# Sparse-attention scores as two rounded products over 128 rows instead of one fp32 product per 64 rows

## The chip, the cores and the metric

The kernel runs on one core of one Trainium2 chip. The metric is the device time of one launch in microseconds (us), the median of several executions. Lower is better.

## The reference

The program is a model of 512 tokens and width 1024, all in fp32. The first block has a gated linear attention layer, a sparse attention layer ("NSA") and a convolutional feed-forward after each. The second block has two layers that mix differential and stick-breaking attention, each with a feed-forward. The change lies in the sparse attention layer, which has 16 query heads in 4 groups, with a head dimension of 64:

```python
q_rot = rope(q, pos)
p_sel = masked_softmax(jnp.einsum('bkgqd,bkqmd->bkgqm', qc, ks) * scale, kpos <= qpos[:, None])
o_sel = jnp.einsum('bkgqm,bkqmd->bkgqd', p_sel, vs)
p_win = masked_softmax(jnp.einsum('bkgqd,bknd->bkgqn', qc, kw) * scale, win_mask)
o_win = jnp.einsum('bkgqn,bknd->bkgqd', p_win, vw)
o = gates[0] * o_cmp + gates[1] * o_sel + gates[2] * o_win
```

At this length the selected blocks and the window both cover every earlier token, so the kernel computes both as plain causal attention, each with keys and values of its own.

## The kernel before, in words

**Weights.** All weight matrices come as a stream of 128x1024 units through a ring of four slots (`w_raw`, filled by SyncE's queue). GpSimd splits each unit (`split`, L496): one cast to the rounded type `w_hi` (L502), then four subtractions of 128x256 that give the remainder `w_lo` (L505). A projection is then three products in the rounded type fp32r: high by high, high by low, low by high (`product`, L544 to L548). For the eight units of the compression network ScalarE does the cast (L1463) and GpSimd only the subtractions. TensorE starts a unit of the attention stages when half of its remainders are there (`unit_rows`, L550).

**The key and value stage** (about 600 to 694 us in the trace) multiplies twelve tiles of 128 columns. VectorE evacuates each (L2116), the four key tiles are rotated (L2133 to L2141, into `n_rot`), and ScalarE writes each half of 64 partitions of a rotated key tile to both halves of the partitions of `n_kk` (`k_doubled`, L1479 to L1485). VectorE also writes the remainders of the next stage's input here (`mixed_low`, L2091). Between the tiles stand the eight compression units (`compress`, L860 to L862). Counted in the order of the stream (`KV_UNIT`, `CMP_UNIT`, L72), units 0 to 6, 8, 10, 12, 14 and 16 are tiles and the rest up to 19 are compression; unit 20 is the first of the query stage.

**The query stage** (694 to about 753 us) multiplies one unit of gates and eight of queries. Each query tile `e` holds two heads, one on partitions 0 to 63 and one on 64 to 127 (`par` 0 and 1). VectorE rotates it into `n_q[:, e]`.

**The score stage** (745 to about 897 us) is a pipeline over 96 score rows. `row(m)` (L207) names each: tile `e = m // 12`, a block of 128 tokens `i`, which of the two sides (selected, window), and the head `par`. Within a tile the rows come in six pairs, by m modulo 12: 0 and 1 have i = 0 and both sides, 256 columns; 2 to 5 have i = 3 and one side, 512 columns; 6 and 7 have i = 1 and both sides, 512 columns; 8 to 11 have i = 2 and one side, 384 columns. For a pair q, q+1:

- TensorE: `scores(q)` (L933) multiplies the two heads' queries with the keys, each on its own 64 rows of the array, in fp32 (L947; every fp32 product is two instructions in the trace), and adds the causal mask (L951). It waits until the exponentials of row q-3 are done (the banks form a ring of four). Then it transposes rows q-4 and q-3 (`transposed`, L953 to L965), each only when the copy of the row three before it has freed its bank (`copied`, L925). At four steps of a tile it multiplies with the values (L1023), once after a product for the compressed part (L1018).
- VectorE, in the order of its loop over q (L2286): copies of odd transposed rows (L2310), the row maximum (L2231), the reciprocal of row q-1's sum (L2237), and now and then other work.
- ScalarE, in its loop (L1578): copies of even transposed rows (L1589, row q-5), the exponentials of row q (L1555), once a tile the rounded output `n_oh` (L1597).
- GpSimd multiplies a row with its gate and reciprocal (`weigh`, L511 to L519) and does no splitting meanwhile.

The order on each engine is written out by hand.

Of the kernel before, what the change touches and what calls it, by code (L numbers as in the profile page):

```python
# [138 lines left out]
def build(nc, x_in, weights, params, consts, masks, gain_out, out):  # L139
    ctx = ExitStack()  # L140
    with ctx:
# [60 lines left out]
        CS_BANK = (6, 7, 6, 0)  # L202
        CMP_TURN_ROW = (22, 58)
        SWAP_ROW = (27, 28, 33, 34, 51, 52, 57, 58)
        PV_ROW = {12 * e + at_: 4 * e + k for e in range(8) for k, at_ in enumerate((10, 12, 14, 16))}
# [40 lines left out]
        def parts_gain(n, k):  # L246
# [50 lines left out]
        o_kh, o_kl = o_A + 4352, o_A + 8448  # L297
        n_kk = at("n_kk", [P, 2, NSA_KV, T], F32, o_kh)
        n_k = [[n_kk[:, c, g, :] for g in range(NSA_KV)] for c in range(2)]
        n_v = [at(f"n_v{s}", [P, TT, NSA_KV * DH], F32, o_A + 12544 + 1024 * s) for s in range(2)]  # L300
# [7 lines left out]

        n_q = at("n_q", [P, 8, T], F32, o_XH)

        n_hid = at("n_hid", [P, 2, 2, P], F32, o_N + 2048)
# [104 lines left out]
            "xh2", "xl2", "kd", "evac", "yh", "yl", "rot", "rope", "vT", "vc", "hid", "kvc", "kvcc", "gT",  # L416
            "gate", "p0", "cs", "csub", "cmax", "ce", "p", "s", "mx", "exp", "w", "t", "tc", "pT", "pTc", "pv", "oh", "o", "rc", "tcd")}
        hs = {n: sem("hyb_" + n) for n in (
# [31 lines left out]
        def _(sp):  # L450
# [13 lines left out]
            rounds = UNITS // RING  # L464
            kv_round, q_round = (START["kv"] + 4) // RING, -(-START["nsa_q"] // RING)

# [12 lines left out]
            refill_rounds(1, kv_round)  # L479
            for u in range(kv_round * RING, q_round * RING):  # L480
                refill(u)
            refill_rounds(q_round, rounds)
            for u in range(rounds * RING, UNITS):
# [11 lines left out]
        def _(pool):  # L495
# [15 lines left out]
            def weigh(m):  # L511
# [7 lines left out]
                ins.then_inc(ns["w"], 1)  # L519

            def split_first():

                for p in range(4):
                    rows, last = slice(2 * p, 2 * p + 2), p == 3
                    if p == 0:
                        pool.wait_ge(s_first_raw, 16)
                    if p == 2:
                        pool.wait_ge(s_raw[0], 16)
                    nc.gpsimd.tensor_copy(w_hi[0][:, rows, :], w_raw[0][:, rows, :]).then_inc(s_hi if last else s_first_hi, 1)
                    pool.wait_ge(s_hi, 1) if last else pool.wait_ge(s_first_hi, p + 1)  # L530
                    nc.gpsimd.tensor_tensor(w_lo[0][:, rows, :], w_raw[0][:, rows, :], w_hi[0][:, rows, :].bitcast(F32),
                                            ALU.subtract).then_inc(s_w if last else s_first_w, 1)

            split_first()
            for u in range(1, UNITS):
                if u == START["nsa_o"] + RING - 1:
                    for m in range(POOL_ROWS, NSA_ROWS):
                        weigh(m)
                split(u)


        @block.tensor
        def _(pe):
# [292 lines left out]
            def nsa():  # L836
# [96 lines left out]
                def scores(q):  # L933

                    e, i, cs, _, n = row(q)
                    S = (i + 1) * P
                    if q >= 4:
                        pe.wait_ge(ns["exp"], q - 2)
                    elif q == 2:
                        pe.wait_ge(ns["csub"], 3)  # L940
                    if q % 12 == 0:
                        pe.wait_ge(ns["rope"], 4 + e + 1)
                    side = slice(cs[0], cs[-1] + 1)
                    for par in range(2):
                        r = slice(DH * par, DH * (par + 1))
# [23 lines left out]
                for t in range(U_NSA_Q):  # L969
# [15 lines left out]
                    if t == 7:  # L985
                        pe.wait_ge(s_bf, 2)
                        pe.wait_ge(ns["kd"], 4)
                        pe.wait_ge(ns["pTc"], 1)
                        scores(0)
# [293 lines left out]
        def _(act):  # L1283
# [163 lines left out]
            def nsa():  # L1447
# [22 lines left out]
                def k_swap(m):  # L1470
                    t = (4, 5, 8, 9)[m]
                    act.wait_ge(ns["evac"], t + 1)
                    if m >= 2:
                        act.wait_ge(ns["kd"], m - 1)
                    half_swap(n_rot[m % 2], n_raw[:, t % 2, :], ns["rot"])

                halves = (slice(0, DH), slice(DH, P))

                def k_doubled(m):  # L1479

                    act.wait_ge(ns["rope"], m + 1)
                    for e, r in enumerate(halves):
                        for to in halves:
                            ins = nc.scalar.activation(n_k[m // 2][2 * (m % 2) + e][to, :], n_rot[m % 2][r, :], ACT.Copy)
                    ins.then_inc(ns["kd"], 1)  # L1485
# [30 lines left out]
                act.wait_ge(ns["kvc"], 1)  # L1516
                act.wait_ge(ns["p0"], 1)
                for par in range(2):
# [23 lines left out]
                def swap(e):  # L1542
                    act.wait_ge(ns["evac"], U_NSA_KV + 1 + e + 1)
                    act.wait_ge(ns["rope"], 4 + e - 1) if e >= 2 else act.wait_ge(ns["kd"], e + 3)
                    half_swap(n_rot[e % 2], n_raw[:, (e + 1) % 2, :], ns["rot"])
# [237 lines left out]
        def _(dve):  # L1783
# [302 lines left out]
            def nsa():  # L2086
# [82 lines left out]
                V.memset(n_bd[:, :, :, :], 0.0).then_inc(ns["p0"], 1)  # L2169
                evac(8)  # L2170
                mixed_low(6)
                evac(9)
# [3 lines left out]
                key(3)  # L2176
                evac(11)

                dve.wait_ge(s_used, CMP_UNIT[-1] + 1)
# [53 lines left out]
                def score_weights(m):  # L2233
# [4 lines left out]
                    if m < POOL_ROWS:  # L2238
# [47 lines left out]
                for q in range(3, NSA_ROWS + 9):  # L2286
# [376 lines left out]
```

## Time and profile before

| | |
|---|---|
| median of 3 executions | 2813.29 us (2812.91 to 2813.4) |
| the profiled execution: its span, first to last instruction | 2810.2 us |
| its own time by the clock of the runs | not noted apart; the median is 3.1 us above the span |
| TensorE busy | 2791.2 us, 99% |
| VectorE, ScalarE, GpSimd busy | 1325.6, 816.3, 2045.0 us |
| granted TensorE clock, mean | 0.999 of full |

Busy times count modelled ends of pipelined matmuls, so an engine at 99% can still be waiting between two starts. The starts in the timeline show that better: the distance from one start to the next is what a matmul really takes from the stream. "idle before" in a row is the time between two spans, and the name behind the arrow is what ended it.

### The profile page before, as it was taken

What the parts mean: (1) busy time and instruction counts of PE and PEld (TensorE: products, weight loads), DVE (VectorE), ACT (ScalarE), POOL (GpSimd) and SP (SyncE); (2) the same over time, 40 slices, a digit from 0 to 9 for tenths busy, and PEclk for the clock granted to TensorE, in tenths of its full rate; (3) what the DMA queues carried; (4) which work ended last, traced back from release to release, by engine and by line L of the source; (5) the groups of instructions that cost most, each with busy time, mean ns of one, the idle gap of its engine ahead of it and who ended that gap; (6) DMA issues with size and microseconds to landing.
All of it is one profiled execution on the core that took longest, in us unless ns stands there. A gap on an engine that the chain in (4) does not pass through costs nothing.

```text
span 2810.2 us, 39309 instructions
## 1 busy us (share of the span) xinstructions
PE 2791.2 (99%) x14380; PEld 2253.4 (80%) x14380; DVE 1325.6 (47%) x1878; ACT 816.3 (29%) x1470; POOL 2045.0 (73%) x2353
## 2 busy tenths in 40 slices
PE   9999999999999999999999999999999999999999
PEld 7888888888766888888877788888887777888887
DVE  4945666044675566604764553321074545432201
ACT  3242222024575222202444422110043444211101
POOL 7958988778654899877845587777785456877774
PEclk9999999999999999999999999999999999999999
DMA  4213323323100333322221233323332222333322
GB/s 154 77 54 105 97 96 94 95 96 128 61 2 8 98 97 97 97 96 91 83 68 61 68 98 98 97 96 93 96 97 70 65 66 77 98 97 95 94 96 96
DMA packets 66507, 242.59 MB, mean 86 GB/s; under 512 B 7504, under 2 KB 7632, under 8 KB 66384
## 3 DMA queue, kind: packets, MB, share of 16 engines
q1 hardware_dynamic: 66384, 240.95, 27.1%
q8 instruction: 78, 1.28, 0.2%
q14 instruction: 45, 0.37, 0.0%
HBM read 238.82 MB, written 2.10 MB: 86 GB/s over the span
## 4 chain that ended last, share of the span: by engine, by line
PE 95%; DVE 2%; ACT 2%; issue 1%; DMA 0%; POOL 0%; SPq 0%; DVEq 0%; ACTq 0%
PE bank L546 28%; PE bank L548 28%; PE bank L547 28%; PE bank L1023 1%; PE bank L947 1%; PE bank L1204 1%; PE bank L1120 1%; PE bank L965 1%; PE bank L1163 1%; PE bank L1176 1%; PE bank L1101 1%; ACT n_P L1555 0%; PE bank L602 0%; PE bank L951 0%; PE bank L1091 0%
## 5 line engine op out<-in xcount | busy, mean ns | idle before, releaser
L505 POOL TENSOR_TENSOR w_lo<-w_raw,w_hi 128x256 fp32r<-128x256 f32 x1780 | 1479.1, 862 | 45.6 <-ACT w_hi L1463 10.6
L546 PE MATMUL bank<-XH,w_hi 128*128 128x512 f32 x2416 | 955.4, 395 | 2.2 <-DVE X L2509 1.6
L548 PE MATMUL bank<-XH,w_lo 128*128 128x512 f32 x2416 | 941.2, 390 | 0.0
L547 PE MATMUL bank<-XL,w_hi 128*128 128x512 f32 x2416 | 940.7, 389 | 0.0
L502 POOL CAST w_hi<-w_raw 128x1024 fp32r<-128x1024 f32 x437 | 486.6, 1114 | 618.0 <-DMA w_raw<-weights_dram 617.4
L546 PEld LDWEIGHTS bank<-XH,w_hi 128*128 128x128 f32 x2416 | 453.6, 188 | 103.1 <-issue 9.3
L548 PEld LDWEIGHTS bank<-XH,w_lo 128*128 128x128 f32 x2416 | 453.4, 188 | 96.3
L547 PEld LDWEIGHTS bank<-XL,w_hi 128*128 128x128 f32 x2416 | 453.8, 188 | 93.4 <-issue 2.6
L1822 DVE TENSOR_TENSOR X<-X,bank 128x512 f32<-128x512 f32 x63 | 43.1, 684 | 511.6 <-PE bank L548 511.3
L548 PE MATMUL bank<-hid_h,w_lo 128*128 (+1 forms) x704 | 273.9, 389 | 0.0
L546 PE MATMUL bank<-hid_h,w_hi 128*128 (+1 forms) x704 | 273.9, 389 | 0.0
L547 PE MATMUL bank<-hid_l,w_hi 128*128 (+1 forms) x704 | 273.9, 389 | 0.0
L1855 DVE TENSOR_TENSOR f_c<-bank,rstd 128x512 f32<-128x512 f32 x88 | 60.9, 692 | 296.5 <-PE bank L548 286.7
L1349 ACT ACTIVATE hid_h<-f_h 128x512 f32 x88 | 55.6, 632 | 392.5 <-DVE f_h L1870 392.5
L547 PEld LDWEIGHTS bank<-hid_l,w_hi 128*128 128x128 f32 x704 | 132.1, 188 | 27.6
L548 PEld LDWEIGHTS bank<-hid_h,w_lo 128*128 128x128 f32 x704 | 132.1, 188 | 27.4
L546 PEld LDWEIGHTS bank<-hid_h,w_hi 128*128 128x128 f32 x704 | 132.1, 188 | 27.3
L518 POOL TENSOR_SCALAR n_P<-n_P,n_st,n_gate 128x512 f32<-128x512 f32 (+3 forms) x124 | 78.7, 639 | 65.8 <-DVE n_st L2237 65.0
L1341 ACT ACTIVATE f_c<-f_u,par_sb 128x512 f32<-128x512 f32 x88 | 71.9, 818 | 168.2 <-DVE f_u L1855 168.2
L1347 ACT ACTIVATE f_s<-f_c 128x512 f32<-128x512 f32 x88 | 55.7, 633 | 197.3 <-DVE f_c L1855 152.3
L1872 DVE TENSOR_TENSOR hid_l<-f_h,hid_h 128x512 f32 x88 | 74.0, 840 | 81.0 <-ACT hid_h L1349 81.0
L1864 DVE SCALAR_TENSOR_TENSOR f_c<-f_u,par_sb,f_c 128x512 f32<-128x512 f32 x88 | 102.6, 1166 | 12.7 <-DVE f_c L1861 0.3
(368 smaller groups left out, 3297.3 us busy)
## 6 DMA issues: line engine op xcount, KB each, us to landing
w_raw<-weights_dram SPq DMA_DIRECT2D x445, 512.0 KB, 3.5
x_tok<-x_dram SPq DMA_DIRECT2D x4, 512.0 KB, 5.4
out_dram<-y_tok SPq DMA_DIRECT2D x4, 512.0 KB, 4.1
const_sb<-consts_dram SPq DMA_DIRECT2D x1, 834.0 KB, 11.8
par_sb<-params_dram SPq DMA_DIRECT2D x1, 665.0 KB, 10.3
masks_in<-masks_dram SPq DMA_DIRECT2D x1, 640.0 KB, 12.9
w_raw<-weights_dram SPq DMA_DIRECT2D x2, 256.0 KB, 6.5
y_gain<-gain_out_dram SPq DMA_DIRECT2D x1, 512.0 KB, 4.5
```

What stands on the lines that cost most here:

```text
L502: nc.gpsimd.tensor_copy(w_hi[s][:, :, :], w_raw[s][:, :, :]).then_inc(s_hi, 1)
L505: ins = nc.gpsimd.tensor_tensor(w_lo[s][:, rows, :], w_raw[s][:, rows, :], w_hi[s][:, rows, :].bitcast(F32), ALU.subtract)
L518: ins = nc.gpsimd.tensor_scalar(w, w, n_st[:, 1, st:st + 1], n_gate[:, i, col:col + 1], ALU.mult, ALU.mult)
L546: nc.tensor.matmul(out_ap, w_hi[slot][:, j, :], xh, start=start, stop=False)
L547: nc.tensor.matmul(out_ap, w_hi[slot][:, j, :], xl, start=False, stop=False)
L548: return nc.tensor.matmul(out_ap, w_lo[slot][:, j, :], xh, start=False, stop=stop)
L1341: nc.scalar.activation(f_c[side][:, :], f_u[side][:, 2:T + 2], ACT.Identity, bias=par_sb[:, bass.ds(t + b0, 1)], scale=par_sb[:, bass.ds(t ...
L1347: nc.scalar.activation(f_s[:, :], f_c[0][:, :], ACT.Silu).then_inc(s_silu, 1)
L1349: nc.scalar.activation(hid_h[:, bass.ds(i * (2 * T) + p * T, T)], f_h[:, :], ACT.Copy)\
L1855: V.tensor_tensor(dst, bank[2 * p + side][:, :], rstd[:, :], ALU.mult).then_inc(s_u, 1)
L1864: V.scalar_tensor_tensor(f, f_u[side][:, 0:T], par_sb[:, bass.ds(c + w0, 1)], f, ALU.mult, ALU.add).then_inc(s_c2, 1)
L1872: V.tensor_tensor(hid_l[:, bass.ds(i * (2 * T) + p * T, T)], f_h[:, :], hid_h[:, bass.ds(i * (2 * T) + p * T, T)].bitcast(F32), ALU.subtract)\
```

## The change

- The keys are kept as two tiles, `n_kh` (rounded, fp32r, written by ScalarE's doubling copy in place of `n_kk`) and `n_kl` (their remainders, written by VectorE, four subtractions of 64x512 for each of four key tiles). ScalarE's half swaps wait for them (`ns["kl"]`).
- The queries of one head are stacked on 128 rows in `n_qs`: GpSimd casts the query tile to both places (`query_parts`, two casts of 128x512 a tile), and VectorE overwrites the other head's 64 rows with this head's remainders (`query_low`, two subtractions of 64x512 a tile).
- A score is then two fp32r products over 128 rows, stacked queries by high keys and stacked queries by low keys, for each of the two heads.
- `query_parts` stands on GpSimd after the splits of the query stage's sixth and eighth unit and before `weigh` of rows 4, 16, 28, 40, 56 and 74. `query_low` stands on VectorE after the rotation of tile 4, after the last evacuation of the query stage, and in its loop at q = 10, 22, 34, 46, 62 and 80.
- SyncE's refills are written out, not looped, up to the output projection. The semaphore `p0` goes.

```diff
-        n_kk = at("n_kk", [P, 2, NSA_KV, T], F32, o_kh)
-        n_k = [[n_kk[:, c, g, :] for g in range(NSA_KV)] for c in range(2)]
+        n_kh = at("n_kh", [P, 2, NSA_KV, T], F32R, o_kh)
+        n_kl = at("n_kl", [P, 2, NSA_KV, T], F32R, o_kl)
...
+        n_qs = at("n_qs", [P, 4, 2, T], F32R, o_XL)
...
+            def query_parts(e):
+
+                pool.wait_ge(ns["rope"], 4 + e + 1)
+                if e >= 4:
+                    pool.wait_ge(ns["s"], 12 * (e - 3))
+                nc.gpsimd.tensor_copy(n_qs[:, e % 4, 1, :], n_q[:, e, :])
+                nc.gpsimd.tensor_copy(n_qs[:, e % 4, 0, :], n_q[:, e, :]).then_inc(ns["qh"], 1)
...
                     for m in range(POOL_ROWS, NSA_ROWS):
+                        if m in QUERY_ROW:
+                            query_parts(2 + QUERY_ROW.index(m))
                         weigh(m)
                 split(u)
+                if u in (START["nsa_q"] + 5, START["nsa_q"] + 7):
+                    query_parts((u - START["nsa_q"] - 5) // 2)
...
                     if q % 12 == 0:
-                        pe.wait_ge(ns["rope"], 4 + e + 1)
+                        pe.wait_ge(ns["ql"], e + 1)
...
-                        nc.tensor.matmul(o, n_q[r, e, i * P:S], n_kk[r, side, e // 2, 0:S], start=True, stop=False)
+                        queries = n_qs[:, e % 4, par, i * P:S]
+                        nc.tensor.matmul(o, queries, n_kh[:, side, e // 2, 0:S], start=True, stop=False)
+                        nc.tensor.matmul(o, queries, n_kl[:, side, e // 2, 0:S], start=False, stop=False)
...
                     if m >= 2:
                         act.wait_ge(ns["kd"], m - 1)
+                        act.wait_ge(ns["kl"], m - 1)
...
+                def key_low(m):
+
+                    dve.wait_ge(ns["kd"], m + 1)
+                    for e, r in enumerate(halves):
+                        g = 2 * (m % 2) + e
+                        for to in halves:
+                            ins = V.tensor_tensor(n_kl[to, m // 2, g, :], n_rot[m % 2][r, :], n_kh[r, m // 2, g, :].bitcast(F32),
+                                                  ALU.subtract)
+                    ins.then_inc(ns["kl"], 1)
...
                 evac(7)
+                key_low(0)
                 mixed_low(5)
...
                 evac(8)
+                key_low(1)
                 mixed_low(6)
...
                 evac(11)
+                key_low(2)
+                key_low(3)
...
+                def query_low(e):
+
+                    dve.wait_ge(ns["qh"], e + 1)
+                    for par, r in enumerate(halves):
+                        ins = V.tensor_tensor(n_qs[halves[1 - par], e % 4, par, :], n_q[r, e, :], n_qs[r, e % 4, par, :].bitcast(F32),
+                                              ALU.subtract)
+                    ins.then_inc(ns["ql"], 1)
...
                         query(e - 1)
+                    if e in (5, 7):
+                        query_low((e - 5) // 2)
...
+                    if q - 6 in QUERY_ROW:
+                        query_low(2 + QUERY_ROW.index(q - 6))
```

## Rows read from the trace of the kernel before

**Rows 1.** The page: the chain that ended last, by engine
```profile
PE 95%; DVE 2%; ACT 2%; issue 1%; DMA 0%; POOL 0%; SPq 0%; DVEq 0%; ACTq 0%
```

**Rows 2.** Windows: stretch, length, busy PE, PEld, DVE, ACT, POOL, clock, DMA share, GB/s
```profile
640.00:694.00 54.00, 53.52 (x341) 47.94 (x340) 22.97 (x27) 27.43 (x40) 50.25 (x61) 1.00 0.40 128
...
745.00:897.00 152.00, 147.74 (x1262) 94.13 (x1263) 108.17 (x276) 103.55 (x323) 83.37 (x131) 1.00 0.03 9
```

**Rows 3.** Timeline of TensorE, a tile's tight steps: start, length, engine, line, operands
```profile
780.09 0.92 PE L947 MATMUL bank<-n_kk,n_q 64*128 64x384 f32 x4 [0.19 <-ACT n_P L1555]
780.94 0.29 PE L951 MATMUL bank<-masks_bf,ident_bf 128*128 128x128 bf16 x2
...
783.72 0.70 PE L947 MATMUL bank<-n_kk,n_q 64*128 64x256 f32 x4
784.36 0.39 PE L951 MATMUL bank<-masks_bf,ident_bf 128*128 128x256 bf16 x2
784.59 0.82 PE L965 MATMUL bank<-const_sb,n_P 128*128 128x128 f32 x6
```

**Rows 4.** Timeline of TensorE, a step with 512 columns
```profile
806.70 1.13 PE L947 MATMUL bank<-n_kk,n_q 64*128 64x512 f32 x4
807.76 0.29 PE L951 MATMUL bank<-masks_bf,ident_bf 128*128 128x128 bf16 x2
```

**Rows 5.** Timeline of TensorE elsewhere: fp32r products, L1204's of 512, 512, 256, 384, 256 columns
```profile
649.12 0.39 PE L547 MATMUL bank<-XL,w_hi 128*128 128x512 f32 x1
649.35 0.39 PE L548 MATMUL bank<-XH,w_lo 128*128 128x512 f32 x1
...
1504.93 0.75 PE L1204 MATMUL bank<-h_sp_hi,negtri_r 128*128 128x512 f32 x3
1505.52 0.45 PE L1204 MATMUL bank<-h_later_hi,negones_r 128*128 128x384 f32 x2
1505.81 0.22 PE L1204 MATMUL bank<-h_sp_hi,negones_r 128*128 128x128 f32 x1
```

**Rows 6.** Timeline of ScalarE in the same tight steps as rows 3
```profile
782.93 0.58 ACT L1555 ACTIVATE n_P<-bank,n_st 128x384 f32<-128x384 f32 x1 [0.45 <-DVE n_st L2231]
...
783.84 0.60 ACT L1589 ACTIVATE n_PT<-bank 128x512 f32<-128x512 f32 x1 [0.24 <-PE bank L1023]
```

**Rows 7.** Timeline of VectorE where `query_low` comes at q = 22
```profile
781.70 0.67 DVE L2310 COPY n_PT<-bank 128x512 f32<-128x512 f32 x1
782.29 0.55 DVE L2231 TENSOR_REDUCE n_st<-bank 128x1 f32<-128x384 f32 x1
```

**Rows 8.** Timeline of VectorE where `query_low` comes at q = 62
```profile
843.60 0.56 DVE L2310 COPY n_PT<-bank 128x384 f32<-128x384 f32 x1 [1.15 <-PE bank L1023]
```

**Rows 9.** All of VectorE's L2091, remainders with both operands in SBUF: min/median/max ns
```profile
L2091 DVE SCALAR_TENSOR_TENSOR XL<-X,par_sb,XH x8: 741/1217/1350, 628.7 to 672.3; 128x512 fp32r<-128x512 f32 x8
```

**Rows 10.** GpSimd's L505 at 664.5 to 669.4 us, then at 669.7 to 674.1: min/median/max ns
```profile
L505 POOL TENSOR_TENSOR w_lo<-w_raw,w_hi x6: 735/737/741, 664.2 to 668.8; 128x256 fp32r<-128x256 f32 x6
L505 POOL TENSOR_TENSOR w_lo<-w_raw,w_hi x4: 1186/1188/1199, 669.5 to 673.0; 128x256 fp32r<-128x256 f32 x4
```

**Rows 11.** Timelines of the key stage: GpSimd's splits, and TensorE's starts of units 10, 14, 20
```profile
652.62 5.91 POOL L505 TENSOR_TENSOR w_lo<-w_raw,w_hi 128x256 fp32r<-128x256 f32 x8
...
654.52 0.47 PE L546 MATMUL bank<-XH,w_hi 128*128 128x512 f32 x1 [0.34 <-POOL w_lo L505]
...
666.72 3.98 POOL L505 TENSOR_TENSOR w_lo<-w_raw,w_hi 128x256 fp32r<-128x256 f32 x5
...
671.25 0.44 PE L546 MATMUL bank<-XH,w_hi 128*128 128x512 f32 x1
...
691.22 2.80 POOL L505 TENSOR_TENSOR w_lo<-w_raw,w_hi 128x256 fp32r<-128x256 f32 x4
...
693.72 0.47 PE L546 MATMUL bank<-XH,w_hi 128*128 128x512 f32 x1
```

**Rows 12.** Timeline of VectorE in the query stage: what follows the rotation of tile 4
```profile
743.00 0.69 DVE L2216 TENSOR_REDUCE n_cst<-n_sc 128x16 f32<-128x512 f32 x1 [2.21 <-ACT n_sc L1536]
```

More of the change, by code:

```diff
@@ L203, in build @@
         CMP_TURN_ROW = (22, 58)
+        QUERY_ROW = (4, 16, 28, 40, 56, 74)
         SWAP_ROW = (27, 28, 33, 34, 51, 52, 57, 58)
@@ L416, in build @@
             "xh2", "xl2", "kd", "evac", "yh", "yl", "rot", "rope", "vT", "vc", "hid", "kvc", "kvcc", "gT",
-            "gate", "p0", "cs", "csub", "cmax", "ce", "p", "s", "mx", "exp", "w", "t", "tc", "pT", "pTc", "pv", "oh", "o", "rc", "tcd")}
+            "gate", "cs", "csub", "cmax", "ce", "p", "s", "mx", "exp", "w", "t", "tc", "pT", "pTc", "pv", "oh", "o", "rc", "tcd",
+            "kl", "qh", "ql")}
         hs = {n: sem("hyb_" + n) for n in (
@@ L464, in _ @@
             rounds = UNITS // RING
-            kv_round, q_round = (START["kv"] + 4) // RING, -(-START["nsa_q"] // RING)
+            kv_round, o_round = (START["kv"] + 4) // RING, -(-(START["nsa_o"] + RING) // RING)
             def refill(u):
@@ L479, in _ @@
             refill_rounds(1, kv_round)
-            for u in range(kv_round * RING, q_round * RING):
+            for u in range(kv_round * RING, o_round * RING):
                 refill(u)
-            refill_rounds(q_round, rounds)
+            refill_rounds(o_round, rounds)
             for u in range(rounds * RING, UNITS):
@@ L941, in scores @@
                     if q % 12 == 0:
-                        pe.wait_ge(ns["rope"], 4 + e + 1)
+                        pe.wait_ge(ns["ql"], e + 1)
                     side = slice(cs[0], cs[-1] + 1)
                     for par in range(2):
-                        r = slice(DH * par, DH * (par + 1))
                         o = bank[ring[(q + par) % 4]][:, 0:len(cs) * S].rearrange("p (c s) -> p c s", s=S)
-                        nc.tensor.matmul(o, n_q[r, e, i * P:S], n_kk[r, side, e // 2, 0:S], start=True, stop=False)
+                        queries = n_qs[:, e % 4, par, i * P:S]
+                        nc.tensor.matmul(o, queries, n_kh[:, side, e // 2, 0:S], start=True, stop=False)
+                        nc.tensor.matmul(o, queries, n_kl[:, side, e // 2, 0:S], start=False, stop=False)
                     for par in range(2):
@@ L987, in nsa @@
                         pe.wait_ge(ns["kd"], 4)
+                        pe.wait_ge(ns["kl"], 4)
                         pe.wait_ge(ns["pTc"], 1)
@@ L1483, in k_doubled @@
                         for to in halves:
-                            ins = nc.scalar.activation(n_k[m // 2][2 * (m % 2) + e][to, :], n_rot[m % 2][r, :], ACT.Copy)
+                            ins = nc.scalar.activation(n_kh[to, m // 2, 2 * (m % 2) + e, :], n_rot[m % 2][r, :], ACT.Copy)
                     ins.then_inc(ns["kd"], 1)
@@ L1516, in nsa @@
                 act.wait_ge(ns["kvc"], 1)
-                act.wait_ge(ns["p0"], 1)
+                act.wait_ge(ns["evac"], U_NSA_KV)
                 for par in range(2):
@@ L1543, in swap @@
                     act.wait_ge(ns["evac"], U_NSA_KV + 1 + e + 1)
-                    act.wait_ge(ns["rope"], 4 + e - 1) if e >= 2 else act.wait_ge(ns["kd"], e + 3)
+                    act.wait_ge(ns["rope"], 4 + e - 1) if e >= 2 else act.wait_ge(ns["kl"], e + 3)
                     half_swap(n_rot[e % 2], n_raw[:, (e + 1) % 2, :], ns["rot"])
@@ L2166, in nsa @@
                 evac(7)
+                key_low(0)
                 mixed_low(5)
                 V.memset(n_kc[:, :, :, :], 0.0)
-                V.memset(n_bd[:, :, :, :], 0.0).then_inc(ns["p0"], 1)
+                V.memset(n_bd[:, :, :, :], 0.0)
                 evac(8)
+                key_low(1)
                 mixed_low(6)
```

## The prediction

> **What bounds the kernel now.** I read the page first. The chain that ended last is TensorE for 95% of the span [rows 1], so what counts is what TensorE's stream of starts loses or gains. Then the windows of the stages the change touches. In the key stage GpSimd is busy for 50.25 of 54 us and VectorE for 22.97; in the score stage TensorE is busy for 147.74 of 152 us, with VectorE at 108.17 and ScalarE at 103.55 [rows 2]. So the change works where TensorE is nearly full, and pays on two engines: VectorE in both stages, and GpSimd's neighbourhood in the first. Last, the timelines, for how much room each neighbour has at the places of the new work.
>
> **The products.** Before, a pair of rows is four fp32 instructions, two for each head. The heads run beside each other on their 64 rows. From the first to the mask behind them it takes 1.06 us at 512 columns (806.70 to 807.76) [rows 4], 0.85 at 384 (780.09 to 780.94) and 0.64 at 256 (783.72 to 784.36) [rows 3]. After, it is four fp32r products one behind the other. Elsewhere such a product takes 0.23 us at 512 columns, and 384 with 256 take 0.29 together [rows 5]. 512, 512 and 256 take 0.59 [rows 5], which leaves about 0.12 for 256 and so 0.17 for 384. The new pairs take 0.92, 0.68 and 0.48, so a pair gains 0.14, 0.17 and 0.16 us. A tile has three pairs of 512, two of 384 and one of 256, together 0.92, over eight tiles 7.4.
>
> Most of this gain is no shorter arithmetic. At 2.4 GHz, the granted level here, 512 columns four times are 0.85 us in both forms. The mask behind waits until the split rows are empty, about 0.1 to 0.2 us a pair, and that wait goes. The Trainium skill says so too (TensorEngine Tiling (Array Packing), Key Properties): a change of tiling mode drains TensorE. The same skill also speaks against the change (TensorE: Matmul & The Clock Gate, Part 3: Packing small matmuls): products of 64 rows in different row groups run concurrently, which is given up here. The rows show that this is just paid back by one pass for two.
>
> **Not all of it arrives.** The last pair of a tile starts when ScalarE has finished an exponential, after a wait of 0.19 us in the rows [rows 3]. From the mask of pair 6, 7 to the transposes behind pair 10, 11, TensorE follows VectorE's maxima, ScalarE's exponentials and its copies. What the two pairs of 384 gain there is waited away again. I count the first four pairs: 0.16 + 3 x 0.14 = 0.58, times 8 is 4.6. In addition four pairs come behind full-array products (in tiles 0, 2 and 5) and lose the same emptying at their front, 0.1 each (my estimate from the 0.1 to 0.2 above): **minus 5.0 us**. Bounds: 4 below, 7.8 if ScalarE's chain does not hold.
>
> **`key_low` in the key stage.** 16 new instructions of 64x512 with both operands in SBUF. The nearest rows, 128x512, take 741 ns at least and 1217 in the median [rows 9]: the long ones stand beside GpSimd. There GpSimd suffers as well: its subtraction takes 1188 ns instead of 737 [rows 10]. So each `key_low` instruction makes GpSimd 0.45 us late, 7.2 in all, 3.6 in the first two calls and 3.6 in the last two. That costs where GpSimd's slack is smaller.
> - Unit 10 already waits for GpSimd, 0.34 us [rows 11]; two of its subtractions now run beside `key_low(0)`: plus 0.9.
> - Unit 14's half is ready at about 668.2 (two subtractions from 666.72) and is started at 671.25 [rows 11], a slack of 3.1. GpSimd is 3.6 late by then, its half now falls beside the rotation (another 0.9 to 1.5), and TensorE itself is 0.9 late: plus 1.2.
> - Units 18 to 20 have `key_low(2)` and `(3)` above them, 3.6 late. Unit 20's half is ready at 692.6 (691.22 and two of them) for a start at 693.72 [rows 11], a slack of 1.1: plus 2.4.
>
> Together **plus 4.5 us**. Bounds: 0, if instructions on 64 partitions leave GpSimd alone; 8.5, if it loses all of VectorE's instruction. The last is a rule of the Trainium skill (SBUF — State Buffer, Who interferes with whom): an instruction of VectorE with two SBUF inputs and a reading one of GpSimd share a port, and the later blocks fully. By that rule a median of 0.7 us would be lost each time and the sum would be about 8 instead of 4.5; the rows show a loss of 0.45, so the sum goes by the rows.
>
> **`query_low`.** Two instructions a tile, 1.4 us by the lowest of [rows 9], 2.4 by the median.
> - Tile 0: VectorE idles 2.21 us behind the rotation [rows 12]. It hides there: 0. Without the idle time it would cost 1.4.
> - Tile 1, behind the last evacuation: it delays the reciprocal that row 3's weighing needs. 0.3, between 0 and 1.4.
> - q = 22: VectorE goes from the copy (781.70) straight to the maximum (782.29), with no gap [rows 7]. Both move by 1.4 or more. The maximum then ends at 784.22, its exponential (782.93 before, 0.58 long) starts at about 784.3 and ends at 784.9, and ScalarE's copy (0.60 long, at 783.84 before) ends at 785.5 [rows 6, 7]. The second of the two transposes needs that copy. It would have come three transposes of 0.11 after 784.59 [rows 3], less 0.16 gained, at 784.8. So TensorE waits 0.7, or 1.7 with the long instructions. I take 1.1, as GpSimd is busy about half the time there.
> - q = 10, 34, 46 and 80 stand at steps equally dense in the same view: 1.1 each. q = 62: VectorE idles 1.15 us before its copy [rows 8]: 0.
>
> Together 0.3 + 5 x 1.1 = **plus 5.8 us**. Bounds: 0 if other slack takes it, 9.
>
> **The rest**, at nothing: GpSimd's 16 casts. In the query stage they stand behind splits four units ahead of TensorE, and the ring's transfers are what GpSimd waits for there. In the score stage GpSimd works 83.37 of 152 us [rows 2], and the rows weighed behind a cast are needed a step later; bare, a pair of casts would cost about 1.5, two of the nearest rows, 737 ns [rows 10]. ScalarE's doubling keeps its four copies; its added waits for `kl` end before the evacuation it waits for anyway. The first product of a tile now waits for `query_low` instead of the rotation, called 2 to 4 rows or more ahead. SyncE's written-out refills issue the same transfers, behind the same waits.
>
> **Sum.** -5.0 + 4.5 + 5.8 = +5.3. The profiled execution has a span of 2810.2 and I take it as an ordinary one, since the median is 3.1 above it: 2813.3 + 5.3 = 2818.6 us.
>
> **Rivals.**
> - *The insertions are hidden* (the other side). VectorE is busy for 71% of the score stage, and the stalls above are read from one tile; work on 64 partitions may not touch GpSimd. Then only the products count: 2813.3 - 5.0 = 2808.3, or 2805.5 with all of the gain. It decides at a `query_low` pair under about 0.7 us of delay and GpSimd's subtraction staying at 737 ns. Against it: the dense steps and the 1188 ns. Chance 0.17.
> - *One of two harms.* GpSimd's lateness is real and the score stage takes the insertions (2813.3 - 5.0 + 4.5 = 2812.8), or the reverse (2814.1). Chance 0.25.
> - *Both at their upper bounds*, a port held for whole instructions: 2813.3 - 5.0 + 8.5 + 7 = about 2824. By the skill's rule above this is what the key stage would do. Chance 0.13.
> - *The products don't get shorter*: with new stationary operands each 0.23 becomes 0.27, 2818.6 + 5 = 2823.6. Chance 0.05.
>
> **Numbers.** The forecast has 0.40, its own range 2815 to 2822. A measurement of this kernel tells about 0.2%, 5.6 us, from no change. Faster by more than that is below 2807.7: the better half of the first rival and a little, 0.10. Slower, above 2818.9: nearly half of the forecast's case and the last two, 0.38. The rest, 0.52, is within. The range 2807 to 2823 leaves out some 0.18.
>
> **What would show it.** Pairs of 512 at 0.92 to the mask. L505 near 1.19 us beside `key_low`, TensorE's units 10, 14 and 20 waiting for `w_lo`, and the key stage 4.5 us longer. TensorE idle about 1 us in the step behind `query_low` at q = 10, 22, 34, 46, 80. The last pair of a tile waiting longer for an exponential. I am wrong if the key stage keeps its length, if these waits are missing, or if the score stage gets shorter by 5 us or more.

## The result, and the profile after

The changed kernel takes 2822.62 us in the median of 5 runs (2821.38 to 2825.01), the kernel before 2812.91 (2812.11 to 2813.4): a ratio of 1.0036, 95% interval 1.0025 to 1.0046. It is slower by 9.7 us, and the interval is clear of 1. The forecast was 2818.6, 5.3 above its base, with a change within 0.2% as the likeliest outcome, and a range of 2807 to 2823. The time lies just inside its upper end. The profiled execution took 2821.38 with a span of 2819.5, against 2810.2 before.

The chain that ended last, by engine, in the changed kernel; it answers to [rows 1]:

```profile
PE 93%; DVE 2%; ACT 2%; POOL 1%; issue 1%; DMA 0%; SPq 0%; DVEq 0%; ACTq 0%
```

GpSimd now has a share. The windows of the changed kernel (columns as in [rows 2]) say where:

```profile
640.00:694.00 54.00, 51.93 (x325) 46.00 (x323) 37.82 (x40) 26.90 (x39) 52.42 (x56) 1.00 0.39 121
690.00:695.00 5.00, 4.34 (x36) 4.20 (x35) 4.93 (x5) 0.00 (x0) 5.00 (x5) 0.91 0.58 197
695.00:700.00 5.00, 5.00 (x18) 4.22 (x18) 1.87 (x2) 2.58 (x6) 4.84 (x7) 0.50 0.34 110
700.00:705.00 5.00, 5.00 (x22) 4.08 (x21) 0.34 (x1) 0.68 (x3) 4.92 (x7) 0.91 0.00 0
745.00:897.00 152.00, 141.26 (x1213) 107.66 (x1212) 116.70 (x281) 100.16 (x308) 94.67 (x137) 1.00 0.03 11
```

In the key stage TensorE lost busy time (53.52 to 51.93 us) and VectorE gained 15 us. In the score stage TensorE fell from 147.74 to 141.26. And one thing was not looked for: from 694.1 to about 701 us the granted clock is 0.50, the 1.2 GHz level.

The same TensorE instruction in both traces, by its start:

| start of | before | changed | later by |
|---|---|---|---|
| the turn ahead of unit 8 | 619.80 | 619.63 | -0.17 |
| unit 10 | 654.52 | 654.41 | -0.11 |
| unit 14 | 671.25 | 672.22 | 0.97 |
| unit 20 | 693.72 | 697.14 | 3.42 |
| behind the first two query units | 704.71 | 709.90 | 5.19 |
| first pair of scores | 745.34 | 750.41 | 5.07 |
| second pair of scores | 749.20 | 755.44 | 6.24 |
| behind the score stage | 901.32 | 911.16 | 9.84 |

So the key stage costs 5.3 and the score stage 4.7. TensorE in the key stage, changed kernel (timeline, as in [rows 11]):

```profile
654.41 0.47 PE L561 MATMUL bank<-XH,w_hi 128*128 128x512 f32 x1 [0.73 <-POOL w_lo L508]
...
672.22 0.47 PE L561 MATMUL bank<-XH,w_hi 128*128 128x512 f32 x1 [0.57 <-POOL w_lo L508]
...
693.83 0.33 PE L875 MATMUL bank<-n_yh,w_hi 128*128 128x130 f32 x1 [0.66 <-POOL w_lo L508]
...
696.25 1.07 PE L617 MATMUL bank<-const_sb,n_raw 128*128 128x128 f32 x4
697.14 0.76 PE L561 MATMUL bank<-XH,w_hi 128*128 128x512 f32 x1
697.71 0.63 PE L562 MATMUL bank<-XL,w_hi 128*128 128x512 f32 x1
698.13 0.63 PE L563 MATMUL bank<-XH,w_lo 128*128 128x512 f32 x1
```

The three waits are for `w_lo`, at the units that the prediction named. The last two starts are 0.42 apart where 0.23 is the step at full clock. The cause on the two other engines: GpSimd's splits behind 652 us, then VectorE's `key_low(0)` beside them and, ahead of unit 20, its `key_low(3)`:

```profile
652.08 7.73 POOL L508 TENSOR_TENSOR w_lo<-w_raw,w_hi 128x256 fp32r<-128x256 f32 x8
```
```profile
651.24 4.72 DVE L2170 TENSOR_TENSOR n_kl<-n_t,n_kh 64x512 fp32r<-64x512 f32 x4
...
690.95 4.82 DVE L2170 TENSOR_TENSOR n_kl<-n_rot,n_kh 64x512 fp32r<-64x512 f32 x4
```

Eight splits took 5.91 before [rows 11] and take 7.73. Taken one by one, five of them are slow now, at 1.05 to 1.19 us beside `key_low(0)` and the `mixed_low` that follows it, where one was before; the others take 0.74. That is 1.8 us for four more slow splits, the 0.45 each of the prediction.

A step with 512 columns in the changed kernel (timeline of TensorE), to lay beside [rows 4]:

```profile
814.42 0.50 PE L962 MATMUL bank<-n_kh,n_qs 128*128 128x512 f32 x1
814.76 0.39 PE L963 MATMUL bank<-n_kl,n_qs 128*128 128x512 f32 x1
814.99 0.40 PE L962 MATMUL bank<-n_kh,n_qs 128*128 128x512 f32 x1
815.22 0.39 PE L963 MATMUL bank<-n_kl,n_qs 128*128 128x512 f32 x1
815.46 0.28 PE L967 MATMUL bank<-masks_bf,ident_bf 128*128 128x128 bf16 x2
```

From the first product to the mask it is 1.04, against 1.06 before and 0.92 forecast. Three of the steps are the expected 0.23; the first is 0.34. The fp32 pair of [rows 4] has its second instruction of each head here:

```profile
807.24 0.59 PE L947 MATMUL bank<-n_kk,n_q 64*128 64x512 f32 x2
```

So its two steps are 0.54 (from 806.70) and 0.52 (to the mask at 807.76). With the prediction's 0.85 us for the streaming, 0.43 a step, there is about 0.1 too much in the first step and 0.1 in the last: the old form too has a slow start, and only the rest stands in front of the mask.

Where `query_low` stands at q = 22, VectorE and then TensorE (timelines, to lay beside [rows 7] and [rows 3]):

```profile
788.77 1.39 DVE L2282 TENSOR_TENSOR n_qs<-n_q,n_qs 64x512 fp32r<-64x512 f32 x2
790.08 0.68 DVE L2354 COPY n_PT<-bank 128x512 f32<-128x512 f32 x1
790.68 0.54 DVE L2263 TENSOR_REDUCE n_st<-bank 128x1 f32<-128x384 f32 x1
```
```profile
791.49 0.49 PE L981 MATMUL bank<-const_sb,n_P 128*128 128x128 f32 x3
792.62 0.52 PE L981 MATMUL bank<-const_sb,n_P 128*128 128x128 f32 x3 [0.64 <-ACT n_PT L1607]
```

That is the forecast's picture: the transposes of the second row wait for ScalarE's copy, which was late because the maximum was. At q = 10, 46 and 80 the wait (0.54, 1.20 and 0.99 us) ends with another engine. At q = 46, TensorE, GpSimd and VectorE:

```profile
831.42 0.52 PE L981 MATMUL bank<-const_sb,n_P 128*128 128x128 f32 x3 [1.20 <-POOL n_P L521]
```
```profile
830.32 1.79 POOL L521 TENSOR_SCALAR n_P<-n_P,n_st,n_gate 128x384 f32<-128x384 f32 x2 [0.98 <-DVE n_st L2269]
```
```profile
827.57 1.39 DVE L2282 TENSOR_TENSOR n_qs<-n_q,n_qs 64x512 fp32r<-64x512 f32 x2
...
830.05 0.16 DVE L2269 RECIPROCAL n_st<-n_st 128x1 f32<-128x1 f32 x1
```

The transposes wait for GpSimd's `weigh`, which waits for a reciprocal that stands on VectorE behind `query_low`, a copy and a maximum. And a stall that was not foreseen, at the second pair of scores, TensorE and then VectorE:

```profile
755.44 0.50 PE L962 MATMUL bank<-n_kh,n_qs 128*128 128x512 f32 x1 [1.32 <-DVE n_sc L2233]
```
```profile
746.00 2.17 DVE L2282 TENSOR_TENSOR n_qs<-n_q,n_qs 64x512 fp32r<-64x512 f32 x2
...
753.24 1.55 DVE L2159 TENSOR_TENSOR n_q<-n_rot,n_t 128x512 f32<-128x512 f32 x1
754.71 0.68 DVE L2233 TENSOR_TENSOR n_sc<-bank,const_sb 128x512 f32<-128x512 f32 x1
```

`query_low(0)` filled the 2.21 us hole of [rows 12], but took 2.17 beside GpSimd's splits. What follows it on VectorE runs with no idle time to speak of up to the subtraction at 754.71, for which TensorE waits.

### The profile page after: what moved, and what is told of

Its sections match the earlier page's. It is cut to its first block, busy times and chain, and to the rows that moved or that the text cites. A ratio compares the mean times of both kernels' runs of the same rounds, so it can differ in the third digit from the quotient of the medians.

```text
span 2819.5 us, 39322 instructions
## 1 busy us (share of the span) xinstructions
PE 2792.8 (99%) x14380; PEld 2272.5 (81%) x14380; DVE 1357.1 (48%) x1910; ACT 816.6 (29%) x1470; POOL 2074.4 (74%) x2369
## 4 chain that ended last, share of the span: by engine, by line
PE 93%; DVE 2%; ACT 2%; POOL 1%; issue 1%; DMA 0%; SPq 0%; DVEq 0%; ACTq 0%
PE bank L561 28%; PE bank L563 27%; PE bank L562 27%; PE bank L1040 1%; PE bank L1221 1%; POOL w_lo L508 1%; PE bank L1137 1%; PE bank L1180 1%; PE bank L1193 1%; PE bank L1118 1%; PE bank L981 1%; PE bank L962 1%; ACT n_P L1573 1%; PE bank L617 0%; DVE n_st L2263 0%
## 5 line engine op out<-in xcount | busy, mean ns | idle before, releaser
L505 POOL CAST w_hi<-w_raw 128x1024 fp32r<-128x1024 f32 x437 | 485.0, 1110 | 607.1 <-DMA w_raw<-weights_dram 606.5
L521 POOL TENSOR_SCALAR n_P<-n_P,n_st,n_gate 128x512 f32<-128x512 f32 (+3 forms) x124 | 85.4, 693 | 57.3 <-DVE n_st L2269 55.9
```

Of the source, the lines that this page charges most:

```text
L505: nc.gpsimd.tensor_copy(w_hi[s][:, :, :], w_raw[s][:, :, :]).then_inc(s_hi, 1)
L521: ins = nc.gpsimd.tensor_scalar(w, w, n_st[:, 1, st:st + 1], n_gate[:, i, col:col + 1], ALU.mult, ALU.mult)
```

## The experiments

The runs were made in three sessions, with the kernel before timed in each (medians 2812.39 for e1 to e4, 2812.0 for e5 to e8, 2812.28 for e9 and e10); differences below are against those.

**e1, the kernel before with `key_low` alone.**

```diff
                 evac(7)
+                key_low(0)
...
                 evac(11)
+                key_low(2)
+                key_low(3)
```

> The kernel before with nothing added but the sixteen subtractions of key_low, written to a buffer that nobody reads, and the waits for them. Theory A (GpSimd is made late by VectorE's two-operand instructions, TensorE waits for its halves at units 10, 14 and 18 to 20, and the clock falls behind those stalls): 5.2 us above the kernel before, of which about 1.8 at halved clock near 695 to 701 us. Theory B (the loss of the key stage comes from something else in the change, so that key_low alone is hidden): within 0.5 us of the kernel before. The sum on record said 4.5.

Measured: 2819.06, 6.7 above (ratio 1.0024, 1.0014 to 1.0034). In its trace TensorE is 5.7 us late at the end of the key stage, through the same units, and only 0.05 more behind the whole score stage. Theory A holds, though the median is 1.5 above its 5.2 (the nine executions lie between 2816.3 and 2821.6), and B falls: the harm of this stage is `key_low`'s.

**e2, the changed kernel without `query_low`.**

```diff
-                        pe.wait_ge(ns["ql"], e + 1)
+                        pe.wait_ge(ns["qh"], e + 1)
...
-                    if e in (5, 7):
-                        query_low((e - 5) // 2)
...
-                    if q - 6 in QUERY_ROW:
-                        query_low(2 + QUERY_ROW.index(q - 6))
```

> The changed kernel without query_low: the queries' remainders are left out, the rows that they would fill hold what was there before, and TensorE waits for GpSimd's casts instead. Theory A (the score stage loses its time behind query_low at six places, 0.7 to 1.4 us each, and 1.2 at the third pair of tile 0): 4 to 5.5 us below the changed kernel, the key stage unchanged at 5.2 late. Theory B (the score stage loses it in the products, which are no shorter, or in the casts on GpSimd): less than 1 us below.

Measured: 2817.0, 4.6 above the kernel before, so 5 below the changed one (e9: 9.7 above). TensorE is 4.45 late behind the key stage and 3.66 behind the score stage: the products with all their casts gain 0.8, and `query_low` alone cost 4.65 + 0.8 = 5.4. Theory A, at its upper end; by the medians it is 5.1.

The key stage of this run also answers another question. TensorE at unit 20 (timeline):

```profile
698.16 0.47 PE L561 MATMUL bank<-XH,w_hi 128*128 128x512 f32 x1 [1.74 <-issue]
698.47 0.39 PE L562 MATMUL bank<-XL,w_hi 128*128 128x512 f32 x1
698.70 0.40 PE L563 MATMUL bank<-XH,w_lo 128*128 128x512 f32 x1
```

Here the same stalls stand and the clock stayed at 1.0 (steps of 0.23). The view names no releaser for the 1.74, but the second of this unit's splits ends at 698.06, and the first weight load starts at 698.13. Without its fall the waits are 0.42 at unit 10, 1.08 up to unit 14 and 2.86 at units 18 to 20, 4.4 in all. Where it falls, it replaces part of the wait at unit 20 and costs about 1 us on top. The profiled execution, 2814.89, is one of the fastest of this run, 2.1 below its median, so its full clock need not be the usual case.

**e3, the changed kernel without either remainder.**

```diff
-                        nc.tensor.matmul(o, queries, n_kl[:, side, e // 2, 0:S], start=False, stop=False)
+                        nc.tensor.matmul(o, queries, n_kh[:, side, e // 2, 0:S], start=False, stop=False)
...
-                key_low(0)
...
-                        query_low((e - 5) // 2)
```

> The changed kernel with neither query_low nor key_low: the remainders of queries and keys are left out and the second product reads the rounded keys again, so TensorE's four products of a pair and GpSimd's sixteen casts stay. Theory A (a pair gains only 0.03 to 0.06 us to its mask, with 0.04 to 0.2 more where it follows full-array work): 1.5 to 2.5 us below the kernel before. Theory B (a pair gains the 0.14 to 0.17 that the sum on record took): 5 below the kernel before. Theory C (the casts cost what the products gain): equal to the kernel before.

Measured: 2811.96, 0.4 below (ratio 0.9998, 0.9989 to 1.0007). Theory B, the sum on record, falls; A is right in kind and still too high. By the time alone theory C could hold as well, but the trace has TensorE wait for GpSimd in the score stage once, for 0.3 us, as before. The score stage is 0.75 shorter and the parts of that can be read. Pairs of 512 gain 0.02 to 0.03 to the mask, of 384 some 0.05, of 256 0.06. The first pair of 384 in a tile gains 0.17 more at its front, where the emptying behind the transposes is gone (its first product starts 0.80 behind the first of the eight transposes, at 776.47, instead of 0.97). But behind it stands this (timeline of TensorE; before, the eight transposes at 778.68 ran without a wait):

```profile
778.18 0.61 PE L981 MATMUL bank<-const_sb,n_P 128*128 128x128 f32 x4
779.01 0.63 PE L981 MATMUL bank<-const_sb,n_P 128*128 128x128 f32 x4 [0.23 <-ACT n_PT L1605]
779.83 0.45 PE L962 MATMUL bank<-n_kh,n_qs 128*128 128x384 f32 x1 [0.19 <-ACT n_P L1571]
```

ScalarE's copy takes the whole 0.23 back. The pairs behind full-array products in tiles 2 and 5 fare alike: the one at q = 26 reaches its mask 0.21 sooner, and 0.19 of that is gone at the next mask, behind a wait of 0.23 for another copy of ScalarE (788.86). About 0.1 a tile is left. The timeline of the weight loads shows where the missing gain of a pair went:

```profile
809.23 0.19 PEld L962 LDWEIGHTS bank<-n_kh,n_qs 128*128 128x128 f32 x1 [0.17 <-ACT n_P L1571]
809.34 0.19 PEld L963 LDWEIGHTS bank<-n_kh,n_qs 128*128 128x128 f32 x1
809.57 0.19 PEld L962 LDWEIGHTS bank<-n_kh,n_qs 128*128 128x128 f32 x1
```

The first load starts with the first product (809.23), all later ones a product ahead. I read the longer first step as this load on the path, about 0.1 us, which the fp32 form pays as well (its first step of 0.54 above). e6 tests how the 0.21 divides.

**e4, `key_low(2)` and `(3)` late.**

```diff
                 evac(11)
-                key_low(2)
-                key_low(3)
...
                 V.tensor_tensor(n_raw[:, 0, :], bank[0][:, :], rstd[:, :], ALU.mult).then_inc(ns["evac"], 1)
+                key_low(2)
+                key_low(3)
```

> The changed kernel with the eight subtractions of key_low(2) and key_low(3) moved on VectorE behind the evacuation of the first query unit, past the scaled cosine. Theory A (these eight made TensorE wait at units 18 to 20, and that wait brought the fall of the granted clock): 3.5 to 4.3 us below the changed kernel, units 18 to 20 without the wait and the granted clock at 1.0 near 695 to 701 us. Theory B (GpSimd is as late whenever they run, since its splits fill the query stage too): the stall appears a few units later and less than 1 us is gained. Theory C (the clock falls there for another reason): 2.4 below, the fall stays.

Measured: 2817.54, 5.1 above the kernel before and 4.5 below the changed one, a little more than expected. TensorE and VectorE (timelines):

```profile
696.33 0.47 PE L561 MATMUL bank<-XH,w_hi 128*128 128x512 f32 x1
```
```profile
702.69 4.11 DVE L2170 TENSOR_TENSOR n_kl<-n_t,n_kh 64x512 fp32r<-64x512 f32 x4
706.83 4.85 DVE L2170 TENSOR_TENSOR n_kl<-n_rot,n_kh 64x512 fp32r<-64x512 f32 x4
```

Unit 20 starts without a wait and the clock is 1.0 there; the subtractions are as slow as ever, and nobody waits for the splits beside them. Theory A. This profiled execution was already 1.05 late at 619 us (the clock was 0.83 from 10 to 20 us), so its key stage lost 1.6: units 10 to 14 alone.

**e5, `query_low` moved as well.**

```diff
-        QUERY_ROW = (4, 16, 28, 40, 56, 74)
+        QUERY_ROW = (8, 20, 32, 44, 56, 68)
...
-                    if e in (5, 7):
-                        query_low((e - 5) // 2)
+                    if e in (2, 5):
+                        query_low(e // 4)
```

> The changed kernel with key_low(2) and key_low(3) late, as in e4, and with query_low at other places of VectorE's stream: tile 0 behind the second rotation, tile 1 where tile 0 was, tiles 2 to 7 at q = 14, 26, 38, 50, 62 and 74 (casts and the last rotation moved to suit), the place in a tile at which q = 62 cost nothing. Theory A (the harm is where the work stands, not that it is done): the stalls of 0.6 to 1.4 us at tile 0's third pair and at q = 10, 22, 46 and 80 go, units 10 to 14 keep their 1.5 us, so 1.3 to 2.3 above the kernel before. Theory B (VectorE has no room in this stage and any place costs 0.7 to 1.4): 5 above the kernel before.

Measured: 2815.68, 3.7 above (1.0002 to 1.002), between the theories, and the trace says why. VectorE in the middle of the stage, then TensorE at the second pair:

```profile
810.06 0.17 DVE L2269 RECIPROCAL n_st<-n_st 128x2 f32<-128x2 f32 x1 [0.47 <-ACT n_P L1573]
810.26 1.39 DVE L2282 TENSOR_TENSOR n_qs<-n_q,n_qs 64x512 fp32r<-64x512 f32 x2
811.57 0.55 DVE L2354 COPY n_PT<-bank 128x384 f32<-128x384 f32 x1
```
```profile
753.13 0.79 PE L962 MATMUL bank<-n_kh,n_qs 128*128 128x512 f32 x1 [2.57 <-DVE n_sc L2233]
753.73 0.63 PE L963 MATMUL bank<-n_kl,n_qs 128*128 128x512 f32 x1
```

All six calls of the score loop now cost nothing (against e3 TensorE is 4.8 us late at 760 us and 5.0 behind the stage): theory A there. But `query_low(1)` took 2.56 us in a hole of 1.8 (VectorE's idle time there in e7), TensorE waited 2.57, and the clock fell behind it (the next step is 0.6 and then 0.42); in this execution it had stayed at 1.0 in the key stage.

**e6, the heads beside each other again, without remainders.**

```diff
-                    for par in range(2):
-                        queries = n_qs[:, e % 4, par, i * P:S]
-                        nc.tensor.matmul(o, queries, n_kh[:, side, e // 2, 0:S], start=True, stop=False)
-                        nc.tensor.matmul(o, queries, n_kh[:, side, e // 2, 0:S], start=False, stop=False)
+                    for k in range(3):
+                        for par in range(2):
+                            nc.tensor.matmul(o, n_qs[r, e % 4, 0, i * P:S], n_kh[r, side, e // 2, 0:S],
+                                             start=k == 0, stop=False)
```

> As e3 (remainders of queries and keys left out), but with the heads beside each other on their 64 rows again, as three fp32r products each, and one cast a tile instead of two. It measures where the 0.21 us of a pair that is not streaming lies. Theory A (0.105 is the load of the first stationary operand, which every form pays, and only 0.104 is the emptying of the split rows in front of the mask): a pair of 512 columns takes 0.105 + 3 x 0.234 + 0.104 = 0.91 us to its mask, and the kernel is 3.5 to 4.5 us below the kernel before. Theory B (split rows cost the whole 0.21, and the 0.1 at the first stacked product belongs to fp32r): 1.01 to 1.02 us, and about 1 us below the kernel before. Theory C (fp32r products on 64 rows don't run beside each other): 0.105 + 6 x 0.234 = 1.5 us, and 8 us or more above.

Measured: 2809.19, 2.8 below (ratio 0.9985, 0.9976 to 0.9994). TensorE (timeline):

```profile
809.96 0.96 PE L962 MATMUL bank<-n_kh,n_qs 64*128 64x512 f32 x6
810.86 0.28 PE L967 MATMUL bank<-masks_bf,ident_bf 128*128 128x128 bf16 x2
```

0.90 to the mask, theory A's 0.91 and neither 1.01 nor 1.5. The steps inside are 0.335, 0.235 and 0.33, the last with the emptying. So the 0.21 us in which a pair does not stream is half at its start and half the emptying. The gain, 2.8 by the medians and 3.3 by the length of the score stage in the trace, is below A's 3.5: the pairs of 384 wait for ScalarE here too. The form also shows what the Trainium skill holds against the change (TensorE: Matmul & The Clock Gate, Part 3: Packing small matmuls): products of 64 rows in different row groups run at the same time. Six of them take three steps here, and the stacked form needs four for the same scores.

**e7, that form with every remainder, on e5.**

```diff
+                    for part, keys in ((0, n_kh), (0, n_kl), (1, n_kh)):
+                        for par in range(2):
+                            nc.tensor.matmul(o, n_qs[r, e % 4, part, i * P:S], keys[r, side, e // 2, 0:S],
+                                             start=part == 0 and keys is n_kh, stop=False)
...
+                    V.tensor_tensor(n_qs[:, e % 4, 1, :], n_q[:, e, :], n_qs[:, e % 4, 0, :].bitcast(F32),
+                                    ALU.subtract).then_inc(ns["ql"], 1)
```

> e5 with the form of e6, all remainders computed: high by high, high by low, low by high on 64 rows for both heads at once, so query_low is one subtraction on 128 rows instead of two on 64, and the cast one instead of two. Nothing of the reference is left out but the product of the two remainders. Theory A: e5 less 3 to 4 us for the products, so 1 to 2 us below the kernel before, the first version here that would beat it. Theory B of e6: at e5's time or 1 below it.

Measured: 2809.48, 2.5 below the kernel before (ratio 0.9991, 0.9981 to 1.0, so only just told from it) and 6.2 below e5, more than the 3 to 4 expected. The rest is e5's stall at the second pair, which is gone: with half the instructions the work fits. All eight of them (first and last start, min, median and max ns):

```profile
L2281 DVE TENSOR_TENSOR n_qs<-n_q,n_qs x8: 671/671/1219, 723.9 to 860.5; 128x512 fp32r<-128x512 f32 x8
```

One on 128 rows costs 671 ns; the changed kernel's on 64 rows had a median of 686 and there were two a tile.

**e8, `key_low` with half the instructions, on e7** (lines ending in "..." are shortened).

```diff
                         g = 2 * (m % 2) + e
-                        for to in halves:
-                            ins = V.tensor_tensor(n_kl[to, m // 2, g, :], n_rot[m % 2][r, :], ...
+                        ins = V.tensor_tensor(n_kl[r, m // 2, g, :], n_rot[m % 2][r, :], ...
...
+                def k_crossed(m):
...
+                        ins = nc.scalar.activation(n_kl[halves[1 - e], m // 2, g, :], n_kl[r, m // 2, g, :].bitcast(F32), ACT.Copy)
```

> e7 with key_low as two subtractions for each key instead of four, straight rows only, and ScalarE copying the remainders to the crossed rows. Eight two-operand instructions of VectorE instead of sixteen stand beside GpSimd's splits. Theory A (GpSimd's lateness goes by the count of these instructions, 0.45 each): the 1.5 us lost at units 10 to 14 falls by half or more, 0.8 to 1.5 us below e7. Theory B (it goes by how long VectorE works there, or ScalarE's four further copies a pair of keys make the rotations late): within 0.3 us of e7 or above it.

Measured: 2808.24, 3.8 below the kernel before (ratio 0.9987, 0.9978 to 0.9996) and 1.2 below e7, theory A. TensorE at units 12 and 14, and the window of the run's beginning:

```profile
665.84 0.48 PE L560 MATMUL bank<-XH,w_hi 128*128 128x512 f32 x1
...
674.02 0.44 PE L560 MATMUL bank<-XH,w_hi 128*128 128x512 f32 x1
```
```profile
10.00:20.00 10.00, 8.00 (x26) 6.33 (x27) 8.30 (x14) 6.51 (x11) 9.60 (x15) 0.66 0.94 387
```

Neither unit waits. Against e7 and counted from the unit before, these two are 0.34 and 0.71 us sooner, 1.05 together; the 0.45 at unit 10 is left. The eight splits behind unit 10's cast take 6.82 here (7.73 in the changed kernel, 5.91 before). The whole span of the profiled execution hides this gain, as it was 2.4 late by 620 us, with the clock at 0.66 in its first 20 us.

**e9, the changed kernel again**, without an edit.

> The changed kernel itself once more, on the chip and in the rounds of the next run. Theory A (the granted clock falls behind the stalls at units 18 to 20, often but not always: it did in two of the three profiled runs that have these stalls, and in none of the six without them): 9 to 10.5 us above the kernel before, a key stage 3.4 to 4.5 us longer by waits, and in this profile either another 1.4 to 1.8 at a lower clock or none. Theory B (the fall belongs to that one run): waits alone, and a median some 8 above.

Measured: 2821.93, 9.7 above (ratio 1.0033, 1.0021 to 1.0046). The clock fell at the same place, 0.59 from 695 to 700 us and 0.72 from 700 to 705. Of four profiled executions with the stalls at units 18 to 20 (the changed kernel, e1, e2, e9) three have the fall; of the eight others none has it there. Theory A. What decides in e2 stays open.

**e10, the stacked products with all their harm moved away.** It is e5 with e8's `key_low`, `query_low(1)` no longer behind the fifth query unit, and:

```diff
                     if q == 7:
+                        query_low(1)
                         cmp_scores(3)
```

> The stacked products of the change with every remainder computed, and all that the runs so far found to remove its harm: key_low in two subtractions a key with ScalarE's crossed copies as in e8, the last two keys late, query_low as in e5 but tile 1's moved from behind the fifth query unit to q = 7, ahead of the last compressed scores, where VectorE idled 1.95 us in e2. Theory A (the stacked products are worth only 0.75 us, and none of the remainder work has to cost TensorE anything but 0.2 at unit 10): 0 to 0.7 below the kernel before, level with e3. Theory B (subtractions on 64 rows, twice as many as e7's, don't fit in the score stage): 1 to 3 above it.

Measured: 2812.57 against 2812.28, ratio 1.0 (0.999 to 1.0009). In the trace it loses 0.4 at unit 10 and 0.3 in the score stage against e3, so it is level with the kernel before and not below it. Theory A in kind: all remainders fit, and the stacked products bring nothing that a measurement can tell.

## Why the prediction was wrong, and where it was right

- **The products, -5.0: this is the step that failed.** e3 and e2 show -0.75 to -0.8. The mechanism was seen, its size was not. "The new pairs take 0.92" was four steady steps of 0.23 without the slow first one; a pair takes 1.04. With the mask's wait of "about 0.1 to 0.2 us a pair, and that wait goes", the sum put most of the 0.21 us of [rows 4] down to the emptying, of which half is the slow start that both forms pay (the steps of the fp32 pair, e3's loads, e6's steps). A pair of 512 gains 0.025, not 0.14. The allowance that ScalarE takes back the gain on the 384s was right in its effect, not in its path. The last pair of a tile waits no longer for its exponential (2.1 us in eight waits in e3, 1.9 in eight before); it is the waits for ScalarE's copies that grow, from 1.8 us in three to 3.5 in ten. Of the 0.4 counted for pairs behind full-array products the front gain is there in tiles 2 and 5, and is taken back the same way (e3, q = 26). The rival that the products don't get shorter had the right size for the wrong reason: the steady step stayed at 0.23, not 0.27.
- **`key_low`, +4.5: right, with some luck in the total.** Without the fall of the clock 4.4 (e2), and unit by unit 0.42, 1.08 and 2.86 for the 0.9, 1.2 and 2.4 forecast, so half a microsecond too much at the first and too little at the last cancel. GpSimd's 0.45 us for each slow split held to the hundredth. The Trainium skill's rule of a full block (SBUF — State Buffer, Who interferes with whom), 0.7 a time and about 8 in all, did not. Instructions on 64 rows harm as much as the 128-row ones of [rows 10]: a split wholly beside them takes 1.17 to 1.19 us, against 1.19 there.
- **The clock was not in the sum.** Behind TensorE's waits at units 18 to 20, and in e5 at 753 us, the lower level followed in four of five profiled cases (the changed kernel, e1, e9, e5; not e2). Behind the 0.73 and 0.57 at units 10 and 14 it never did, nor behind waits of 1.20 to 1.38 us in the score stage (the changed kernel, e4, e9). So the stalls go before the fall, and what decides about it is not shown. Net it cost about 1 us in the key stage.
- **`query_low`, +5.8: right in its sum (5.4), not in every place nor in every path.** Only q = 22 waits for ScalarE's copy, as worked out; q = 10, 46 and 80 wait for the reciprocal and `weigh` behind it. In time, q = 22 took 0.83, q = 10 0.74, q = 46 1.4, q = 80 1.0, and q = 62 nothing, as said. q = 34, put down for 1.1, was free. Tile 0, put at nothing, cost 0.6 through the second pair of scores, and tile 1 took 0.7 instead of 0.3. "It hides there" had the bare 1.4 in mind; beside GpSimd's splits it is 2.17 of a 2.21 us hole.
- **The rest at nothing: right.** e2 and e3, both with all sixteen casts, lie within 0.05 us of each other over the whole score stage, and TensorE's one wait for GpSimd there, 0.3 us, is the one of the kernel before. No run takes the casts out alone.

In sum -0.8 + 5.3 + 5.4 = 9.9, against 9.7 measured. Had the products been sized at 0.8, the same working would have given 2822.8; it would still have owed that to a clock at nothing and a `query_low` 0.4 too dear, which partly cancel.

## What to carry over

Before trading a matmul's form for another, split the time from its first start to the next instruction into slow start, streaming and emptying, each from its own row; what both forms pay is no gain. Two-operand work of VectorE had its price on GpSimd's side by the count of instructions here (0.45 us each), so halve the instructions (full 128 rows, copies to ScalarE) and put them where nobody waits for GpSimd's product. Here that, with the heads left side by side as three fp32r products, turned a loss of 9.7 us into a gain of 3.8 (e8, 0.04 to 0.22% below the kernel before).

## What was unexpected about the hardware

- Six fp32r products on 64 rows ran as three side by side, 0.90 us for 512 columns to the mask, against 1.06 for the fp32 pair and 1.04 for four stacked ones (e6).
- The granted clock can fall to 0.50 right after TensorE has waited for another engine, and stay there for some 7 us (694.1 to about 701), but need not: e2 waited longer, 1.74 at unit 20 alone, and kept 1.0.
- GpSimd's `weigh` of 128x384 took 1.69 us beside `query_low`'s two subtractions on VectorE (770.09 and 827.64 in the changed kernel) and 0.66 in the kernel before (781.88). TensorE did not wait for these, since the next `weigh` stood waiting for its reciprocal.
- The clock was also at 0.66 to 0.83 from 10 to 20 us in five of the twelve profiled executions (e4, e6, e8, e9, e10), which made TensorE 1.1 to 2.4 us late by 620 us. A single execution of these kernels can't tell 2 us; the starts around the edit can tell 0.1.
